# A two-layer hybrid encoder: banded attention placed beside the projection chunks, weight splits moved to GpSimd

## The reference

```
h = rmsnorm(x);  proj = h @ w_in            # 25 column chunks of 128
A: B * dwconv3(C * h_A)
B: latent attention, 4 heads, all 1024 keys, low-rank q/kv, rotary part
C: u = va*sigmoid(vb); dwconv31(u); layernorm; silu; @ w_pw
D: banded attention, 4 heads (2 kv heads), keys within +-128, bias, sink
each group * silu(gate);  out = concat @ w_out;  x = x + rmsnorm(out)
```

## Time and profile before

| | |
|---|---|
| median of 3 runs | 2498.44 us (2498.14 to 2498.53) |
| the profiled execution | 2496.92 us |
| its span in the trace | 2495.1 us |
| PE busy | 2278.4 us, 91% |
| DVE busy | 1597.5 us, 64% |
| ACT busy | 1016.4 us, 41% |
| POOL busy | 81.2 us, 3% |
| granted clock, mean | 0.968 of full |

### The profile page before, as it was taken

One profiled execution on the slowest core, in us unless ns is written; L12 is line 12 of the kernel. 1 busy time (PEld: TensorE's weight loads), 2 busy tenths in 40 slices (PEclk: granted clock), 3 DMA queues, 4 the chain that ended last, 5 costly groups with the idle time before them and its releaser, 6 DMA issues.

```text
span 2495.1 us, 28675 instructions
## 1 busy us (share of the span) xinstructions
PE 2278.4 (91%) x11474; PEld 1896.3 (76%) x11474; DVE 1597.5 (64%) x2127; ACT 1016.4 (41%) x1741; POOL 81.2 (3%) x128
## 2 busy tenths in 40 slices
PE   6999977989999996888999999688899999869888
PEld 5888866778888885677888887567788888767777
DVE  4259487984426948797532794879653288487953
ACT  3211265762321127576332113757532211376741
POOL 1000010000000000000100001000010000100000
PEclk8999989999999998999999999899999999989999
DMA  4211000015211100002421110000332111000022
GB/s 170 68 39 59 30 1 18 1 60 194 93 51 47 51 22 1 17 9 78 178 91 51 47 43 22 18 1 18 128 135 85 51 47 47 9 18 1 26 76 85
DMA packets 38804, 136.31 MB, mean 55 GB/s; under 512 B 4720, under 2 KB 5232, under 8 KB 38672
## 3 DMA queue, kind: packets, MB, share of 16 engines
q1 hardware_dynamic: 38672, 134.47, 15.9%
HBM read 116.63 MB, written 17.83 MB: 54 GB/s over the span
## 4 chain that ended last, share of the span: by engine, by line
PE 72%; DVE 17%; ACT 6%; issue 3%; DMA 1%; SPq 0%; POOL 0%; POOLq 0%; ACTq 0%
PE ps L512 44%; PE ps L778 13%; PE ps L727 3%; DVE bnb L1483 2%; DVE PTb L1196 2%; PE ps L762 2%; PE ps L742 2%; DVE woR L1196 1%; PE ps L522 1%; ACT Pd L1016 1%; PE ps L647 1%; PE ps L279 1%; DVE PTd L1196 1%; PE ps L656 1%; PE ps L624 1%
## 5 line engine op out<-in xcount | busy, mean ns | idle before, releaser
L512 PE MATMUL ps<-hT,stat 128*128 128x512 f32 x4416 | 1010.0, 390 | 0.0
L512 PEld LDWEIGHTS ps<-hT,stat 128*128 128x128 f32 x4416 | 827.5, 188 | 173.3 <-issue 1.9
L778 PE MATMUL ps<-woR,catR 128*128 128x512 f32 x1536 | 365.7, 399 | 22.0 <-DVE catR L1196 13.3
L778 PEld LDWEIGHTS ps<-woR,catR 128*128 128x128 f32 x1536 | 292.8, 192 | 86.8 <-DVE catR L1196 14.1
L1263 DVE SCALAR_TENSOR_TENSOR accC<-uC,parT,accC 128x1024 f32<-128x1024 f32 x240 | 290.3, 1278 | 0.0
L1196 DVE TENSOR_TENSOR stat<-raw,stat 128x1024 fp32r<-128x1024 f32 x92 | 112.3, 1221 | 133.7 <-ACT stat L897 133.3
L897 ACT ACTIVATE stat<-raw 128x1024 fp32r<-128x1024 f32 x92 | 97.0, 1054 | 215.6 <-PE ps L512 215.3
L1483 DVE TENSOR_REDUCE bnb<-ps 128x1 f32<-128x1024 f32 x128 | 156.1, 1220 | 35.6 <-PE ps L727 34.7
L903 ACT ACTIVATE th<-ps 128x1024 f32<-128x1024 f32 x40 | 41.1, 1028 | 334.5 <-PE ps L512 334.5
L1196 DVE TENSOR_TENSOR PTb<-ps,PTb 128x512 fp32r<-128x512 f32 x256 | 163.7, 680 | 19.9 <-ACT PTb L1086 19.4
L742 PE MATMUL ps<-ident,Pb 128*128 128x128 f32 x1024 | 135.9, 275 | 42.8 <-ACT Pb L1078 42.3
(11 more groups left out here) (189 smaller groups left out, 2699.6 us busy)
## 6 DMA issues: line engine op xcount, KB each, us to landing
raw<-w_in SPq DMA_DIRECT2D x100, 512.0 KB, 3.5
raw<-w_out SPq DMA_DIRECT2D x32, 512.0 KB, 3.5
y<-xs SPq DMA_DIRECT2D x32, 512.0 KB, 2.6
xs<-x SPq DMA_DIRECT2D x16, 512.0 KB, 3.5
xs<-y SPq DMA_DIRECT2D x16, 512.0 KB, 3.5
xd<-x SPq DMA_DIRECT2D x8, 512.0 KB, 10.4
ropeT<-rope SPq DMA_DIRECT2D x4, 1024.0 KB, 5.9
xd<-y SPq DMA_DIRECT2D x8, 512.0 KB, 10.9
```

The lines of the kernel that those rows point to most:

```text
L512: last = mm(ps[:, 2 * (c % 2) + h, :], w[:, a, k, :], hT[:, h, b, k, :], start=(k == 0 and (a, b) == (0, 0)), stop=(k == KD - 1 and (a, b) ...
L778: last = mm(ps[:, 2 * (n % 2) + h, :], catR[:, n % 2, a, k, :], woR[k][:, b, h * HALF:(h + 1) * HALF], start=(k == 0 and (a, b) == (0, 0)) ...
```

## The change

- **D goes into the projection.** From chunk `D_AT` = 5 on, each of 16 chunks has one unit of D beside it. Within chunk c PE runs `d_scores(u)`, block 0, `d_out(u-1)`, blocks 1 to 4, `d_transpose(u)`, blocks 5 to 7. The buffers of a unit are single: scores in banks 4 and 5, transposes and output in 6 and 7, one `Pd`, one `PTd`. The gates of D come last, and the factor is applied there.
- **Order of the chunks.** The inputs of D come first, its gates move to the end, and the latents `bq0`, `bq1`, `bkv` move forward.
- **Taps.** The 62 operations are spread over 15 chunks by `TAPS_AT`; the first 12 and the last 12 are of one half only, so that each needs the one before it.
- **Weight splits.** The lo part of every chunk, of `w_pw`, `w_q` and `w_kv` is computed by POOL. `w_out` stays on DVE.
- **Buffers.** `RAWS` and `STATS` go from 3 to 2. Q, K and V of D are split straight from PSUM. `w_out6` and `w_out7` have a buffer of their own (`rawX`), and `EARLY` is 5.
- **Behind the chunks** only the up-projections and `pw` are left before B.

```diff
-EARLY = 4
+EARLY = 5
-RAWS = 3
-STATS = 3
+RAWS = 2
+STATS = 2
+ALONE = ("w_out6", "w_out7")
+NU = 2 * NT
+D_AT = 5
+TAPS_AT = dict(enumerate((4, 5, 3, 5, 5, 5, 2, 4, 4, 5, 5, 3, 5, 2, 5), D_AT + 1))
...
+                    def d_scores(u):
+                        n, kv = DU[u]
+                        k0, nk, b0 = keys(n)
+                        if u >= 1:
+                            pe.wait_ge(*got("dm_ok", u))
...
+                    def d_transpose(u):
+                        n, kv = DU[u]
+                        _, nk, _ = keys(n)
+                        pe.wait_ge(*got("de_ok", u + 1))
+                        if u >= 1:
+                            pe.wait_ge(*got("do_ok", u))
...
+                    def d_out(u):
+                        n, kv = DU[u]
+                        k0, nk, _ = keys(n)
+                        pe.wait_ge(*got("dr_ok", u + 1))
+                        pe.wait_ge(*got("dpt_lo", u + 1))
+                        tr(ps[:, 6, 0:P], drx[:, :], ident[:, :])
...
+                    for c, name in enumerate(CHUNKS):
                         halves = (1,) if name in CHUNKS[:2] else (0, 1)
+                        u = c - D_AT
+                        if 0 <= u < NU:
+                            d_scores(u)
+                        project(name, halves, range(0, 1))
+                        if 1 <= u <= NU:
+                            d_out(u - 1)
+                        project(name, halves, range(1, 2))
...
+                        project(name, halves, range(2, 5))
+                        if name == "cvb0":
+                            v_transposes()
+                        if 0 <= u < NU:
+                            d_transpose(u)
...
+                    q_up("rope", GW)
+                    q_up("rope_sw", GW + P)
...
+                    k_up("bk1", P)
+                    q_up("bqn1", P)
+                    k_up("bk0", 0)
+                    q_up("bqn0", 0)
...
+                    def split_lo(name):
+                        i = POS[name]
+                        pool.wait_ge(*got("whi", i + 1 - PRE))
...
+                        pool.tensor_tensor(dst[:, 1], src, dst[:, 0].bitcast(F32), ALU.subtract).then_inc(q["wlo"], 1)
...
+                    for c in range(NC):
+                        u = c - D_AT
+                        if c:
+                            name = CHUNKS[c - 1]
+                            evacuate(name)
...
+                        if 1 <= u <= NU:
+                            d_half(u - 1)
+                        if 0 <= u < NU:
+                            d_exp(u)
+                        if c + 1 in range(PRE, NC):
+                            split_hi(CHUNKS[c + 1])
...
+                        if 0 <= u < NU:
+                            d_hi(u)
...
+                    evacuate("bg1")
+                    dve.wait_ge(*got("ke_hi", 1))
+                    minus(Ke[k_r, 1, :], rawB[k_r, 1, :], Ke[k_r, 0, :]).then_inc(q["ke_lo"], 1)
+                    rope_product(0, "rope")
+                    conformer_gate(0)
+                    rope_product(1, "rope_sw")
+                    conformer_gate(1)
```

More of the change, by code:

```diff
@@ L47 @@
 NEG = -1e30
-EARLY = 4
+EARLY = 5
 B_SCALE = (NOPE + ROPE) ** -0.5
 D_SCALE = HD ** -0.5
[L53 to L56, removed]
+CHUNKS = ["dq0", "dq1", "dk", "dv", "cvb0", "cva0", "cvb1", "cva1", "cg0", "cg1",
+          "ac0", "ah0", "ab0", "ag0", "bq0", "bq1", "bkv", "ac1", "ah1", "ab1", "ag1",
+          "dg0", "dg1", "bg0", "bg1"]
 C = {name: n for n, name in enumerate(CHUNKS)}
 NC = len(CHUNKS)
-LATER = ["dv_t", "pw0", "pw1", "bcast_q", "bcast_kv", "rope", "rope_sw", "bv0", "bv1", "bk0", "bqn0"]
+LATER = ["rope", "rope_sw", "bv0", "bv1", "bk1", "bqn1", "bk0", "bqn0", "pw0", "pw1"]
 for _n, _name in enumerate(LATER):
@@ L317, in before @@
             return q[name], now[0] * TOTAL[name]
[L320 to L321 removed]
+        read_by = {"dq0": ("dst_lo", 2), "dq1": ("dst_lo", 4), "dk": ("kd_lo", 4)}
+        read_by |= {"bv0": ("vb_lo", NT // 2), "bv1": ("vb_lo", NT), "bk0": ("k_lo", 2), "bqn0": ("q_lo", 2)}
         for p in range(2):
@@ new lines, in d_out @@
+                    def d_out(u):
[4 more added lines that the diff above has]
+                        tr(ps[:, 6, 0:P], drx[:, :], ident[:, :])
+                        for b in range(nk):
+                            for part in range(2):
+                                last = mm(ps[:, 7, 256:512], Vd[:, k0 + b, kv, :, :],
+                                          PTd[:, part, b * 2 * P:(b + 1) * 2 * P],
+                                          start=(b == 0 and part == 0), stop=(b == nk - 1 and part == 1))
+                        last.then_inc(q["do_mm"], 1)
@@ L720, in b_scores @@
                         if u < 2:
-                            pe.wait_ge(*free_at(("bqn0", "bk0")[u]))
+                            pe.wait_ge(*free_at(("pw1", "pw0")[u]))
                         if u >= 2:
@@ L1038, in _ @@
-                    NU = len(DU)
-                    for i in range(NU + 3):
-                        if 1 <= i <= NU:
-                            d_hi(i - 1)
-                        if i < NU:
-                            d_exp(i)
-                        if i >= 3 and i % 2:
-                            d_half((i - 3) // 2)
-                        between(i)
+                        if u >= 1:
+                            act.wait_ge(*got("do_mm", u))
+                        act.activation(PTd[:, 0, 0:nk * 2 * P], bank67[:, 0:nk * 2 * P], ACT.Copy).then_inc(q["dpt_hi"], 1)
@@ new lines, in latent_lo @@
+                    def latent_lo(j):
+                        rows, dst = ((P, qlR[:, 0, :, :]), (QR - P, qlR[0:QR - P, 1, :, :]), (P, kvR[:, :, :]))[j]
+                        dve.wait_ge(*got("lat_hi", j + 1))
+                        minus(dst[:, 1, :], rawB[0:rows, j, :], dst[:, 0, :]).then_inc(q["lat_lo"], 1)
+                    taps_done = 0
+                    for c in range(NC):
+                        u = c - D_AT
+                        if 0 <= u < NU:
+                            d_max(u)
+                        if c:
+                            evacuate(CHUNKS[c - 1])
+                        if 1 <= u <= NU:
+                            d_combine(u - 1)
+                        if p == 0 and CHUNKS[c] == "dv":
+                            dve.wait_ge(p_bias, 16)
+                            own.add(dve.tensor_scalar(bias[:, :, :], bias[:, :, :], 1 / D_SCALE, None, ALU.mult))
+                            own.wait()
+                        if c in TAPS_AT:
+                            if taps_done == 0:
```

812 lines of the change are left out of this document (372 added, 440 removed).

## The result

The changed kernel takes 2358.39 us (median of 4 runs, 2357.32 to 2358.73), the kernel before 2498.29 us beside it: ratio 0.944, 95% interval 0.9424 to 0.9456. That is 140 us less; 112 were forecast. The profiled execution took 2358.34 us, with a span of 2356.5. One of the four executions of experiment 8's first kernel, the profiled one, ran at a lowered clock (0.877, 2526.59 us for 2457.36), so its profile is read for what released a wait and for nothing else.

What follows compares the result with a forecast made beforehand. PE bounds the projection, latency bounds D. Per pass (329.7 - 287.6) + (33.7 - 102.8) + 0.9 - 2.1 = -28.2 us, four times -113: from 2496.9 to 2384, median 2386 us; 8-in-10 range 2350 to 2428.

Steps and rivals of the forecast that it cites:

- The main step: Units of D beside projection chunks: 69 us a pass paid with 42 us PE; 2.6 us in hand at `d_transpose`.
- A unit of D: PE's work for one unit in the projection: 2.16 us plus three changes of kind at 0.1, 2.46 us.
- GpSimd's split: One lo part of 128x1024 on POOL beside a chunk: 2.4 us, with 6.9 us of room.
- The rival price of 82 ns a column: Upper reading for POOL's split, from 0.66 us for 8 columns without any fixed part: 84 us.
- the rival of a long split: POOL's split makes PE wait in the chunks; gain gone at about 8.5 us, 2806 us at 12; chance 0.07.
- The lock: DVE taps and POOL splits in the projection make each other wait: 1 us a pass.
- Taps well over 1.28 us: Sign of being wrong, in the chunks: DVE's convolution taps taking much longer than 1.28 us each.
- the rival true, and dearer than its 2474: DVE becomes the bound of the chunks as taps and POOL take turns: 2474 us; chance 0.16, mostly near 2425.
- From the last chunk to B: Stretch between projection and B: 33.7 us instead of 102.8, with PE standing from 9 to 15 us before `bk1`.
- The clock's part: Slower matmuls at a lowered clock after the gap ahead of `bk1`: 2.5 us a pass.
- B: One more split of `w_out` on DVE beside B: 0.9 us more a pass.
- Output: Waits of 0.75 and 1.33 us for `w_out` in the first output block go: -2.1 us a pass.

Runs made afterwards that it cites:

- experiment 8: First kernel: the changed kernel with its 62 taps over the last ten chunks instead of fifteen, GpSimd splits kept; 2457.36 us, ratio 0.9839.
- experiment 5: Changed kernel with small waited-for ACT copies added ahead of each unit's exponentials: fourteen copies 2467.91 us, six copies 2359.48 us.
- experiment 1: Changed kernel with the lo parts of the chunks and `w_pw` back on DVE; 2352.94 us, ratio 0.9424.
- experiment 2: Kernel before with only the lo parts of the chunks and `w_pw` moved to GpSimd; 2498.03 us, ratio 1.0001.
- experiment 3: Changed kernel with each chunk's lo part made twice on GpSimd, same values; 2496.39 us, ratio 0.9993.
- experiment 7: Changed kernel with V's hi and lo parts moved first between the last chunk and B; 2341.19 us, ratio 0.9373.
- experiment 6: Changed kernel with `EARLY` 4 instead of 5, one `w_out` split less beside B; 2358.19 us, ratio 0.9444.

## Why the prediction was right, and where its sizes were off

- **The main step holds.** D's latency is hidden by a projection that PE bounds. The projection is full on PE, the wait total for the loop is 2.6 us, and delays of ACT show its slack at 2.7 us (experiment 5), the prediction's 2.6. The table has the exchange: 69.3 us a pass less between the projection and B, 39.6 more in the projection. That the gain is nothing of the offload is shown from both sides (experiments 1 and 2). The smaller edits that came with the move (the order of the chunks, the buffers, the splits straight from PSUM) were not taken back one by one, so their part is in the table's numbers and is not known.
- **A unit of D** costs 2.26 us, not 2.46: if its matmuls cost the 2.16 that I put, three changes of kind at 0.1 us cost 0.03 us each. That is 3.2 us a pass. What is left of the projection's growth is 3.7 us where 3 were put for waits. Only 0.65 of it were waits (327.4 - 326.75); some 1.5 us is the stretch at clock 0.58, for which I had no term (in experiment 1 a pass with such a stretch took 325.8 us, the two without it 324.3), and the rest stays open.
- **GpSimd's split** takes 2.72 us (2.37 at least) for 2.4. The rival price of 82 ns a column fell: 1024 columns took 2.72 us, and the 128x8 of the earlier trace rows, 0.66 us there, takes less in the changed kernel:

```profile
1454.93 0.24 POOL L840 TENSOR_SCALAR rsq<-brs 128x8 f32<-128x8 f32 x1
```

  The trace of the kernel before suggests why. The operation of the earlier trace rows ended at 1547.54, just behind one of DVE with two SBUF inputs that ended at 1547.44:

```profile
1546.21 1.23 DVE L1347 SCALAR_TENSOR_TENSOR accC<-th,accC 128x1024 f32<-128x1024 f32 x1 [1.19 <-ACT th L903]
```

  So most of the 0.66 us was probably the same waiting that I had read in the earlier trace rows, where L259 took 0.91 us for a median of 0.19, and no price of 8 columns. With this line read, the rival of a long split would have had next to nothing for it.

- **The lock** cost DVE's taps 123 us, 31 a pass. For the pass's time I had put 1 us. With the splits on DVE the projection is 1.6 us shorter in a pass with the slow stretch in both kernels, and 3.1 in the two where only the changed kernel has it (experiment 1), so the splits on GpSimd cost PE little, if more than the 1 us. "Taps well over 1.28 us" was one of my own signs of being wrong, and it came: the time is right because DVE had just the room. My two readings (GpSimd waits, or DVE loses up to 2.4 us) were both too simple: both sides lose, DVE the more. Twice the splits make the rival true, and dearer than its 2474: 2496 us (experiment 3). One more term in the same place was too small: the reciprocals cost 0.95 us each, not 0.4.
- **From the last chunk to B** 33.5 us for 33.7: the chain of DVE operations and the wait at `bk1` came as worked out, the wait 5.25 us for 6. The clock's part is some 1.7 us for 2.5: the six matmuls behind the wait took 2.93 us and the next twelve 3.57, for 1.66 and 3.17 behind a short wait (experiment 7).
- **B** came out at +1.0 for +0.9. But the piece of `w_out` itself costs 1.7 us there (experiment 6), and B's first twelve matmuls took 3.86 us for the 5.17 of the earlier trace rows, which gave back 1.3 and had no term, so the agreement is partly luck.
- **Output** fell by 5.2 us a pass, not 2.1. The waits of the earlier trace rows gave their 2.1. Of the other 3.1 us, 2.5 are the first twelve matmuls, at full rate for half rate (3.01 for 5.49 us), and the rest stays open. No step of mine gave those 2.5, and in four passes they are about 10 us of the 26 by which the profiled time (2358) is under the forecast (2384).

What was mis-sized is thus the sum's small terms: 2.5 us a pass in the projection (329.7 for 327.2) and 3.1 in output (96.2 for 93.1), both on the side of a gain.

## What to carry to other kernels

A phase that is bound by latency from engine to engine can be laid beside a phase that one engine fills; its price is that engine's work alone, as long as each step of the loop has slack, so write down the slack of every step in the busiest chunk, and spread other work around the chunks that have extra. Moving an operation with SBUF inputs to GpSimd did not relieve DVE in the changed kernel, where it fell among operations of DVE with two SBUF inputs (DVE busy 1676.9 us for 1644.3); there, charge DVE for it at full length. It did relieve DVE where it met fewer of them (experiments 2 and 5), so look at what it will stand beside. After a phase is hidden, look at the new order in front of the next one: 17 us lay in which of five hi/lo parts came first.

## What the runs showed of the hardware

- One GpSimd subtraction of 128x1024 beside DVE taps: 2.37 to 3.39 us on GpSimd, and a tap between 1.27 and 3.47 us instead of 1.28. Both sides wait; neither always wins. Without GpSimd's splits the 240 taps take 1.27 to 1.29 us (experiment 1). The Trainium skill ("SBUF — State Buffer", Who interferes with whom) has the exclusion, and this case adds the price, 1.34 us of DVE for a split among taps and none in the taps for a split behind them (experiment 5).
- The output block begins in one of several ways after a wait of 3.32 us: the same twelve matmuls took 5.49 us before and 3.01 to 3.04 after, in all four passes of each. Windows around it, of the kernel before and then of the changed one (PE's busy time ahead of and behind the wait; the granted clock is the number behind POOL's):

```profile
1760.00:1778.00 18.00, 13.69 (x99) 12.26 (x97) 15.42 (x28) 14.49 (x27) 0.00 (x0) 0.97 0.24 84
1778.00:1790.00 12.00, 11.12 (x45) 8.93 (x46) 5.71 (x10) 3.71 (x5) 0.00 (x0) 0.76 0.00 0
```

```profile
1660.00:1679.00 19.00, 13.97 (x100) 12.30 (x98) 16.81 (x29) 15.55 (x28) 0.00 (x0) 1.00 0.17 56
1679.00:1690.00 11.00, 10.90 (x56) 9.33 (x57) 7.23 (x11) 3.71 (x5) 0.00 (x0) 1.00 0.01 1
```

  The granted clock, a mean over 1.2 and 2.4 GHz, was 0.76 in one and 1.00 in the other, with nearly the same work in front. In experiment 1 the output stretch was 95.6, 95.8 and 92.9 us in the first three passes of one kernel. So about 2.7 us a pass can come or go with a shift ahead, some 0.4% of the kernel in four passes. One thing goes with it: in eleven kernels with D beside the projection (all here but the first of experiment 8), B's first twelve score matmuls took 3.8 to 4.0 us in 12 passes, and output's twelve took 3.0 to 3.1 in all of these. In the other 32 passes B's took 3.0 and output's 4.3 to 5.5, but for one with 3.1. So the start of B and that of output, some 126 us later, go together in 43 of 44 passes. What links them, and what decides either, stays open; no run here was made for it.
